# Differential attention in a two-block kernel: the mask product on TensorE replaced by maxima and exponentials over two halves of the query rows

## What is computed

```
CHUNK = 64
Q_BLOCK = 128
def _diff_attention(q, k, v, lam):
    key_chunk = jnp.arange(s) // CHUNK
    def block(args):
        q_blk, start = args
        q_chunk = (start + jnp.arange(Q_BLOCK)) // CHUNK
        mask = key_chunk[None, :] <= q_chunk[:, None]
        sc = jnp.einsum("bqhmd,bkhmd->bhmqk", q_blk, k,
                        preferred_element_type=jnp.float32)
        sc = jnp.where(mask, sc, -jnp.inf)
        p = jax.nn.softmax(sc, axis=-1).astype(v.dtype)
        o = jnp.einsum("bhmqk,bkhe->bqhme", p, v)
        return o[:, :, :, 0] - lam * o[:, :, :, 1]
```

## Time and profile before

| | |
|---|---|
| median of 3 runs | 2320.39 us (2320.14 to 2320.41) |
| profiled execution | 2320.31 us |
| its span | 2318.5 us |
| PE busy | 2312.5 us (100%), 10450 matmuls |
| PE weight loads | 1900.2 us (82%) |
| DVE busy | 1418.3 us (61%) |
| ACT busy | 1115.5 us (48%) |
| POOL busy | 496.6 us (21%) |
| chain that ended last | PE 95%, DVE 2%, ACT 1%, DMA 1% |

### The profile page before, as it was taken

The page is one execution under the profiler, slowest core; times in us unless marked ns, Lnnn a source line. Parts: engine busy times, 40 slices in busy tenths (PEclk is TensorE's granted clock), DMA queues, the critical chain, the costliest instruction groups (busy, mean ns, idle before and its releaser), DMA issues.

```text
span 2318.5 us, 26575 instructions
## 1 busy us (share of the span) xinstructions
PE 2312.5 (100%) x10450; PEld 1900.2 (82%) x10450; DVE 1418.3 (61%) x1947; ACT 1115.5 (48%) x1448; POOL 496.6 (21%) x576
## 2 busy tenths in 40 slices
PE   9999999999999999999999999999999999999999
PEld 7777888888888888888888888888888888888887
DVE  6766766654556555554455556669994766466564
ACT  7433646544435544443344444544556644444653
POOL 1101011310102010010000011149997222022100
PEclk9999999999999999999999999999999999999999
DMA  9675456766445766665566666655555676654454
GB/s 354 197 232 160 156 184 234 238 213 200 165 154 192 244 210 200 207 209 191 199 198 202 208 205 213 207 193 182 185 193 170 207 235 216 194 191 148 161 170 138
DMA packets 253101, 461.05 MB, mean 199 GB/s; under 512 B 19679, under 2 KB 39834, under 8 KB 252273
## 3 DMA queue, kind: packets, MB, share of 16 engines
q1 hardware_dynamic: 238288, 432.13, 56.1%
q0 software_dynamic: 14688, 27.24, 4.3%
HBM read 432.57 MB, written 2.10 MB: 187 GB/s over the span
## 4 chain that ended last, share of the span: by engine, by line
PE 95%; DVE 2%; ACT 1%; DMA 1%; issue 1%; SPq 0%; POOL 0%; DVEq 0%; ACTq 0%
PE ps L97 94%; PE ps L100 1%; DVE WLO L109 1%; ACT WHI L103 0%; SPq L138 0%; DMA RAW<-in_w_in 0%; DMA B<-T 0%; DVE T L117 0%; ACT ps L103 0%; POOL B L138 0%; DVE ED L109 0%; DVE X L109 0%; ACT L103 0%; ACT BB L103 0%; DMA B5b<-T 0%
## 5 line engine op out<-in xcount | busy, mean ns | idle before, releaser
L109 DVE TENSOR_TENSOR WLO<-RAW,WHI 128x1024 fp32r<-128x1024 f32 x701 | 851.3, 1221 | 692.7 <-ACT WHI L103 689.4
L103 ACT ACTIVATE WHI<-RAW 128x1024 fp32r<-128x1024 f32 x793 | 835.8, 1058 | 887.9 <-PE ps L97 881.4
L97 PE MATMUL ps<-WHI,Ahi 128*128 128x512 f32 x1904 | 751.9, 395 | 0.8 <-DVE WLO L109 0.6
L97 PE MATMUL ps<-WHI,Alo 128*128 128x512 f32 x1904 | 741.0, 389 | 0.0
L97 PE MATMUL ps<-WLO,Ahi 128*128 128x512 f32 x1904 | 740.7, 389 | 0.0
L97 PEld LDWEIGHTS ps<-WHI,Ahi 128*128 128x128 f32 x1904 | 357.4, 188 | 78.9 <-issue 3.3
L97 PEld LDWEIGHTS ps<-WLO,Ahi 128*128 128x128 f32 x1904 | 357.5, 188 | 76.2 <-issue 3.3
L97 PEld LDWEIGHTS ps<-WHI,Alo 128*128 128x128 f32 x1904 | 357.4, 188 | 75.0
L109 POOL TENSOR_TENSOR WLO<-RAW,WHI 128x1024 fp32r<-128x1024 f32 x92 | 218.9, 2405 | 53.0 <-ACT WHI L103 52.5
L120 DVE SCALAR_TENSOR_TENSOR ps<-YT,GC,ps 128x256 f32<-128x256 f32 x480 | 188.8, 479 | 8.0 <-ACT ps L103 8.0
L138 POOL DMA_DIRECT2D AC<-TF x88 | 46.3, 534 | 562.0 <-DVE TF L117 559.1
(11 more groups left out here) (327 smaller groups left out, 2228.5 us busy)
## 6 DMA issues: line engine op xcount, KB each, us to landing
RAW<-in_w_gate_up SPq DMA_DIRECT2D x88, 1024.0 KB, 5.1
RAW<-in_a_w_in SPq DMA_DIRECT2D x48, 1024.0 KB, 5.1
RAW<-in_w_down SPq DMA_DIRECT2D x44, 1024.0 KB, 5.0
RAW<-in_w_in SPq DMA_DIRECT2D x39, 1024.0 KB, 6.7
RAW<-in_w_xkv SPq DMA_DIRECT2D x32, 1024.0 KB, 5.7
RAW<-in_w_kv SPq DMA_DIRECT2D x32, 1024.0 KB, 5.9
RAW<-in_b_w_in SPq DMA_DIRECT2D x32, 1024.0 KB, 5.5
RAW<-in_w_out SPq DMA_DIRECT2D x16, 1024.0 KB, 5.1
```

The lines of the kernel that those rows point to most:

```text
L97: return self.e.matmul(o, l, r, start=start, stop=stop, skip_group_check=True)
L103: return self.e.activation(o, i, func, scale=scale, **kw)
L109: return self.e.tensor_tensor(o, a, b, op)
```

## The change

The mask product, the tile `MASK`, its DMA and its copy are gone. The two score products now each open and close their own sums. The maximum and the exponentials are taken apart for rows 0 to 63 (all keys but the last 64) and rows 64 to 127 (all keys). The corner of rows 0 to 63 and the last 64 keys is never written by an exponential any more; it is set to zero once in each of the two buffers, ahead of the maxima of blocks 0 and 1.

```diff
+    def seen_keys(n):
+        nk = P * (n % 2 + 1)
+        return (slice(0, 64), nk - 64), (slice(64, P), nk)
...
-    put(("dk", 2), 0, ("mask",))
...
-            e.wait_ge(*of("mask", 0))
             for mp in range(2):
-                e.matmul(b[:, mp * nk:(mp + 1) * nk], DQT[:, 2 * h + mp, t * P:(t + 1) * P], DKT[:, 2 * h + mp, 0:nk],
-                         mp == 0, False)
-            o = b[:, 0:2 * nk].rearrange("p (m c) -> p m c", m=2)[:, :, nk - P:nk]
-            i = e.matmul(o, MASK[:, 0:P], MASK[:, P:2 * P].unsqueeze(1).to_broadcast([P, 2, P]), False, True)
+                i = e.matmul(b[:, mp * nk:(mp + 1) * nk], DQT[:, 2 * h + mp, t * P:(t + 1) * P], DKT[:, 2 * h + mp, 0:nk], True, True)
...
-            elif what == "mask":
-                e.wait_ge(*of("d_mrow", 0))
-                e.activation(MASK, MROW).then_inc(*done("mask", 0))
...
                 for mp in range(2):
-                    i = e.activation(o[:, mp, 0:nk], v[:, mp, :], AF.Exp, bias=mx[:, mp:mp + 1], accum_out=sm[:, mp:mp + 1])
+                    for r, seen in seen_keys(k):
+                        i = e.activation(o[r, mp, 0:seen], v[r, mp, 0:seen], AF.Exp, bias=mx[r, mp:mp + 1], accum_out=sm[r, mp:mp + 1])
...
-                e.reduce(cols(("dmax", k % 4), 2), pa.ap(("ds", k))[:, 0:2 * nk].rearrange("p (m c) -> p m c", m=2), AL.max, negate=True) \
-                    .then_inc(*done("diff_max", k))
+                mx, v = cols(("dmax", k % 4), 2), pa.ap(("ds", k))[:, 0:2 * nk].rearrange("p (m c) -> p m c", m=2)
+                if k < 2:
+                    e.memset(diff_exps(k)[0:64, :, nk - 64:nk], 0.0)
+                for r, seen in seen_keys(k):
+                    i = e.reduce(mx[r, :], v[r, :, 0:seen], AL.max, negate=True)
+                i.then_inc(*done("diff_max", k))
...
-                if name == ("dk", 0):
-                    e.wait_ge(*full(("co", 3)))
-                    e.dma_start(MROW, C["mask_row"]).then_inc(*landed("d_mrow", 0))
```

More of the change, by code:

```diff
@@ L299, in by_block @@
         return ap.rearrange("p (b c) -> p b c", b=8)
-    MROW, MASK = TMP[:, 768:1024], at("MASK", 121, [256], F32R)[:, :]
     banks = [nc.alloc_psum_tensor(f"ps{i}", [P, 512], F32) for i in range(8)]
@@ L2304, in constants @@
     masks = np.zeros((P, 128), f32)
-    mask_row = np.zeros((P, 256), f32)
-    mask_row[0, 0:64], mask_row[0, 192:256] = 1.0, -1e30
     j, i = np.arange(P)[:, None] % 64, np.arange(64)[None, :]
@@ L2315, in constants @@
     out = {"ident": np.eye(P), "fd": tiles(fd), "fh": fh, "idf": tiles(idf), "fc": tiles(fc),
-           "cc": cc, "alt": alt2, "feats": feats[by_parity].T, "masks": masks, "reset": reset, "mask_row": mask_row}
+           "cc": cc, "alt": alt2, "feats": feats[by_parity].T, "masks": masks, "reset": reset}
     return {k: np.ascontiguousarray(v, dtype=f32) for k, v in out.items()}
```

## The result

The changed kernel takes 2331.84 us (median of 6 runs, 2331.1 to 2332.44) against 2320.39 of the kernel before (6 runs, 2319.99 to 2320.57): 11.45 us more, a ratio of 1.0049 [1.0038, 1.0059]. The forecast of 2324.7 had the sign right and the size wrong, and the range, which ended at 2327.8, did not hold it.

A forecast was written before the change was run, and what follows sets the result against it. PE, busy 100% of the span, was taken to bound the kernel. New waits of 6.24 less 1.92 for the mask products cost 4.32, giving 2324.7 us against the median of 2320.39; range 2321.8 to 2327.8.

The forecast's parts named there:

- the places named: PE waits at transposes of blocks 1, 4, 7, 9, 14, block 13's scores and third-chunk query transposes, 6.24 in all.
- The chain through the query chunks: Delays of blocks 3 and 6 are handed on to blocks 4 and 7, giving waits of 1.96 and 0.93.
- rival 2: Delays not handed on from block 3 to 4 and 6 to 7; waits sum to 3.94, 2322.4; chance 0.14.
- Rival 3: The cover holds: PE meets no new wait and only the mask products count; 2318.5; chance 0.07.
- the price of ACT: Added exponentials on ACT priced by columns alone: +0.60 in an even block, +0.81 in an odd one.
- rival 1: On DVE the second reduce does not overlap the first: 0.09 per chained delay, +0.72, 2325.4; chance 0.20.
- the formulas of the prediction: PE's wait is delay (0.79 even, 1.27 odd) less slack, plus 0.12 per mask product in between; sum 6.24.
- Rival 4: On ACT, instructions starting at other rows don't overlap: 0.1 at 8 borders, 0.8 a block, 2331.1; chance 0.09.
- The sign named for it: Starts of ACT's four exponentials 0.5 or more apart, to be checked if the time is over 2328.
- Rival 5: PE's clock falls to 1.2 GHz after a wait of 1.4 or more; about 5, so 2329.7; chance 0.02.
- whole prices: Upper end: each added instruction priced as a whole one, delays 1.12 and 1.60, memset 0.485; waits 9.21, 2327.7.

The follow-up runs named there:

- the rows in turn: Changed kernel with its exponentials reordered, both maps of rows 0 to 63, then both of rows 64 to 127: 2329.41 us, ratio 1.0036.
- the best of the changed kernel: Changed kernel with that exponential order, and the steps from the transposes on one slot later for blocks 8 to 15: 2325.06 us, ratio 1.0020.

## Why the prediction was wrong

**What held.** The mask products were worth what was said (0.12 each in the traces, 1.63 in all measured alone). The durations were right: 0.309, 0.363, 0.416 and 0.469 for the four exponentials, 0.165 for the memset against 0.16. PE waits at the places named and is let go by the engines named; two waits were not named, 1.34 for ACT at the transposes of the last query chunk, and 0.47 at block 12's transposes. The chain through the query chunks hands a delay on: in the changed kernel DVE stands 1.83 for POOL ahead of scaling ND at 2099.42, where it stood 1.55 before, so rival 2 is out, and block 4 stands far longer than block 14 (2.80 against 1.18). Rival 3 is out with PE idle in all of them.

**The step that failed** is the price of ACT: "rows are worked in parallel in all that it shows, so I take columns alone: 64 columns 0.30, 192 columns 0.41". That is the duration. What a chain pays is the step to the next start, and I took for granted that the 0.1 of overlap at the read of the sum holds between rows 0 and 64. It does not: ACT is later by 1.07 in an even and 1.29 in an odd block, against 0.60 and 0.81. On DVE the second reduce has lost its 0.09 as well (rival 1). With the measured delays, 1.33 and 1.86, the formulas of the prediction, unchanged, give 1.12, 3.09, 2.06, 1.98, 1.24 and 1.27: 10.76, where 10.56 was measured. The way delays add was right in the main, and one price in it was not. But the sum is nearer than its parts: block 1 stands 0.18 and block 4 0.29 less than by formula, block 7 0.31 more. In block 1 a slack was overlooked. Before, DVE was scaling ND until it started `WLO` at 2071.35, 1.34 behind the start of ACT's `WHI`, where 1.09 is enough in block 0. So the first 0.25 of the delay cost nothing: in the changed kernel `WHI` starts 1.86 later and `WLO` 1.61 (2072.96). For block 7 the prediction read the slack at the combination alone and not at the query transposes; whether that is the 0.31 is not shown.

Of the 6.47 by which the profiled execution exceeds its own forecast (2331.10 against 2320.31 + 4.32), 4.32 are waits longer than forecast, 1.6 is the low clock, and 0.55 was not traced.

**Rival 4** was this mechanism, and got 0.09, with the reason that nothing excluded it. Its price was off: it said 0.1 at each of 8 borders, 0.8 a block, and the trace shows it at four, the ones from the read of a sum to the next activation; an exponential and its own read keep theirs. The sign named for it, steps of 0.5 or more, holds in odd blocks (0.52 to 0.59 in block 1) and would have missed it in even ones (0.41 to 0.48). ACT's part over the forecast is 0.47 and 0.48 a block, DVE's 0.07 and 0.11. That rival 4's 2331.1 is close to the measured 2331.84 is in part chance, since it holds nothing of the clock. I gave the loss of overlap on DVE 0.20 and on ACT 0.09, though the two hang together: what had no row for DVE had none for ACT. By the Trainium skill, VectorE: DVE Perf Modes, section Two Vector instructions with no wait between them, an operand that starts in another group of 32 partitions holds the instruction until all earlier ones are done; the trace agrees on DVE, 0.67 for two reduces at rows 0 and 64 against 0.61 with both at row 0 in block 0, and 1.26 against 1.14 in block 1.

**Rival 5**, the clock, got 0.02 and occurred. It is worth 1.6 here, not 5: the low clock lasted for 8 products, not for 24. It was seen in the profiles of five kernels, all with a wait of PE over two microseconds, and in none where the longest in the attention blocks was 1.54 or less (seven experiments and the kernel before). So it probably hangs on the mis-sized delays: the longest wait forecast was 1.96 in all, and near 1.7 in a stretch.

**The range** was built from "whole prices" as its upper end (1.12 and 1.60 for a delay). The measured 1.33 and 1.86 lie above it. A further whole exponential was not an upper bound, since what is lost besides is overlap at the borders of the instructions that were already there.

**What stays open.** Why the clock falls behind one wait over two microseconds and not behind another, and in some runs of a kernel and not in others: behind the same wait of 2.14 at block 4 it fell in the profile with the rows in turn, and not in that of the best of the changed kernel. That the loss of overlap on ACT depends on the start row was tested for rows 0 and 64 alone, and input, output, bias and sum always changed their row together, so which of them does it is not known.

## To carry to other kernels

Splitting an instruction by rows pays its fixed part twice, and alternating between the halves also costs the overlap with the neighbour. So order split instructions so that the same start row comes in a run (here 2.4 us back of 11.45), and price a chain by steps from start to start, with a row of just that pair, or with both prices in the range. The matmul saved here was worth 0.12 on the engine that sets the time; a delay of 1 to 2 in the chain of the small engines is dear against that as soon as the slack is thinner. A wait over two microseconds in a full PE may also cost clock behind it, so add up the delays that are handed on before you size each wait.

## What the hardware showed that was not expected

- ACT starts an activation 0.09 behind the start of the read of a sum before it if both start at the same row (0 to 0 or 64 to 64), and 0.20 behind if the start row changes: steps of 0.31 and 0.36 against 0.41 and 0.46 for 64 and 128 columns.
- A mask product of 128 columns cost 0.10 to 0.11 in the stream of PE, one of 256 columns 0.12 (1.20 and 1.22 in block 1 against the 1.10 without).
- PE's granted clock fell to 1.2 GHz for about 3 us after it had stood for 2.80, and for about 7 us after two waits of 2.02 and 0.77 close together; with 2.14 in another profile it did not fall. Products of 512 columns were then 0.43 apart instead of 0.23. On the page, with slices of 58 us, none of this is seen.
